# Attention items in tile order instead of block order, in a one-core diffusion backbone on Trainium2

## The chip, the cores and the metric

The program runs on one core of one Trainium2 chip. TensorE (PE) multiplies, VectorE (DVE) and ScalarE (ACT) work on the results, GpSimd (POOL) does a few small steps, and SyncE (SP) issues the DMAs. Each engine has a queue of its own that it works through in order; they wait for each other at semaphores. The metric is the time of one execution on the device in microseconds, as the median of the runs.

## The reference, cut to what matters

The reference runs two token streams, 512 latent tokens and 128 context tokens, through four layers. Layers 0 and 3 mix tokens by attention, layer 1 by pooling, layer 2 by a Fourier transform, and each layer ends with a gated ConvFFN. Here only the attention core matters:

```python
def attend_block(qb, keys, values, masks, sink):        # qb: 128 queries
    for kp, mk in zip(keys, masks):
        s = jnp.einsum('bqkgd,bskd->bkgqs', qb, kp) * scale
        if mk is not None: s = jnp.where(mk, s, NEG_INF)
        scores.append(s)
    m = max(sink, max of all scores); denom = exp(sink - m)
    for s, vp in zip(scores, values):
        p = jnp.exp(s - m[..., None])
        denom = denom + jnp.sum(p, axis=-1)
        out = out + jnp.einsum('bkgqs,bskd->bqkgd', p, vp)
    return out / denom
```

There are 16 query heads and 4 key heads of 64 channels. A block of 128 latent queries sees its own block of keys, its neighbours (with a band mask of width 128) and 128 cached context keys. The block of context queries sees only the 128 context keys. The output of the attention goes through a 1024 x 1024 matrix (`attn_w_o`) into the residual stream.

## The kernel before

All activations lie transposed: 1024 channels in 8 tiles of 128 partitions, 642 columns (512 latent, 128 context tokens, and two extra columns). A weight matrix is taken in units of one output tile. Each unit is a sum over 8 (or 11) input tiles, and each input tile is five matmuls on split values (L607 to L611), so that the products are as exact as in fp32.

The attention core of a layer is 40 items: 8 query tiles of two heads each, times 5 blocks of queries (`nb` 0 to 3 latent, `nb` 4 context). `WORK` (L382) lists them, and item `w` of the layer (counted from 0 in this text) is looked up in it by every engine. Before the change the list runs over the tiles within a block: items 0 to 7 are block 0, and so on, and items 32 to 39 are the context block. The size of an item is set by its block alone. `BLOCKS` (L381) holds the key blocks: three for `nb` 0 and 3, four for `nb` 1 and 2, one for `nb` 4. This text calls them 3-block, 4-block and 1-block items. A tile thus has two 3-block, two 4-block items and one 1-block item.

An item goes through a pipeline that is written out by hand, one step of the loop per item and engine, in these orders:

- PE, step w (L876 to L898): `scores(w+1)` (L830, L833), `values(w-3)` (L861), `turn(w-1)`, which transposes the probabilities (L846). In layer 0, for even w from 4 to 30, it multiplies one chunk of the modulation weights as well (`ada_multiply`, L747), and at w = 34 it turns the collected rows (`ada_turn`, L757).
- DVE, step w (L1765 to L1776): `masked(w)` adds the mask and takes the maximum (L1737, twice, then L1744 and L1745), `normed(w-1)` divides by the sum (L1753, then L1755 for two heads), `out_lo(w-4)` makes the low part of the output (L1762). In layer 0 it also copies and adds the modulation rows at w = 33 and 35 (L1408, L1415).
- ACT, step w (L1227 to L1233): `exps(w)` (L1207), `out_hi(w-3)` (L1224), `turned(w-1)` copies the transposed probabilities out of PSUM (L1218).
- POOL puts the sink into a spare column of each probability tile (L589).

The waits that matter: `scores(w+1)` wants `masked(w-1)` finished (L820), since the scores have two pairs of PSUM banks. `masked(w)` wants its scores (L1735). `turn(w-1)` wants `normed(w-1)` (L840). `values(w-3)` wants the output bank free (L853, L854): layer 3 has two output banks (`out_bank`, L413), so the low part of item w-5 must be done; layer 0 has one, since the other holds the modulation sums, so the low part of item w-4 must be done, and DVE does that at the end of its own step w.

The first unit of the output matrix is begun inside the loop. `first_output(kk)` (L866) multiplies input tile kk, and `FIRST_OUTPUT` (L65) says after which step: tiles 0 to 2 at step 39, 3 and 4 at 40, 5 at 41, 6 and 7 at 42. It waits for the low parts of the items that it reads (L871): in block order tile kk is complete with item 32 + kk. The DVE waits once per tile for the scales of the query heads (L1742), in the first eight items.

Of the kernel before, what the change touches and what calls it, by code (L numbers as in the profile page):

```python
# [29 lines left out]
KT = D // P  # L30
# [31 lines left out]
FIRST_PAIRS = FIRST_CHUNKS // 2  # L62
FIRST_BATCHES = FIRST_PAIRS + 1
X_PARTS = ((0, 2), (2, 4), (4, 8))
FIRST_OUTPUT = {39: (0, 1, 2), 40: (3, 4), 41: (5,), 42: (6, 7)}  # L65
IDLE_TILES = {"pool": 17, "fnet": 23}
UP_ROWS = 10
DOWN_PAIRS = (8, 6)
# [37 lines left out]
def build(nc, t):  # L106
    with ExitStack() as ctx:
# [3 lines left out]
        def sem(name):  # L111
            return ctx.enter_context(nc.semaphore(name))
# [181 lines left out]
        ol_made = sem("ol_made")  # L294
# [84 lines left out]
        CACHED = (384, 384, 384, 0)  # L379
        SPAN = ((128, 512), (0, 512), (0, 512), (0, 384), (128, 256))  # L380
        BLOCKS = ((1, 2, 3), (0, 1, 2, 3), (0, 1, 2, 3), (0, 1, 2), (1,))  # L381
        WORK = [(nb, tile) for nb in range(5) for tile in range(KT)]  # L382

        def turns_in(layer, half):

# [161 lines left out]
        def _(pool):  # L547
# [14 lines left out]
            for layer in range(DEPTH):  # L562
                for second in (False, True):
# [9 lines left out]
                    if KINDS[layer] == "attn" and not second:  # L573
# [6 lines left out]
                        for w in range(w0, w0 + 40):  # L580
                            nb, tile = WORK[w - w0]
                            end = SPAN[nb][1]
# [12 lines left out]
        def _(pe):  # L595
            def products(par, kk, b, first, last, plain=False):


                main, wide = ps[:, 2 * par, 0:MAIN], ps[:, 2 * par + 1, :]
                wh, wl = w_hi[par][:, kk, :], w_lo[par][:, kk, :]  # L600
                if plain:
                    for n, (w, part) in enumerate(((wh, 0), (wh, 1), (wl, 0))):
                        pe.matmul(main, w, b[:, part, 0:MAIN], start=(first and n == 0), stop=(last and n == 2))  # L603
                        mm = pe.matmul(wide[:, 0:TAIL], w, b[:, part, MAIN:NT], start=(first and n == 0),  # L604
                                       stop=(last and n == 2))
                    return mm
                pe.matmul(main, wh, b[:, 0, 0:MAIN], start=first, stop=False)  # L607
                pe.matmul(main, wh, b[:, 1, 0:MAIN], start=False, stop=False)  # L608
                pe.matmul(wide, wh, b[:, :, MAIN:NT], start=first, stop=last, skip_group_check=True)  # L609
                pe.matmul(main, wl, b[:, 0, 0:MAIN], start=False, stop=last)  # L610
                return pe.matmul(wide[:, 0:TAIL], wl, b[:, 0, MAIN:NT], start=False, stop=last,  # L611
                                 skip_group_check=True)
# [28 lines left out]
            def h_tiles(kk):  # L641
                return h[:, kk, :, :]
# [144 lines left out]
            for layer, kind in enumerate(KINDS):  # L787
# [5 lines left out]
                if kind == "attn":  # L793
# [20 lines left out]
                    w0 = 40 * a  # L814

                    def scores(w):
                        nb, tile = WORK[w - w0]
                        ga = tile // 4
                        if w - w0 >= 2:
                            pe.wait_ge(max_made, w - 1)  # L820
                        if w - w0 < 2:
                            wait_taken(pe, u0 + 10 + w - w0)
                        pe.wait_ge(qk_ready, 10 * a + tile + 3)
                        for hd in range(2):
                            rows = slice(HD * hd, HD * hd + HD)
                            q = qkv[rows, Q0 + tile, TOKEN_BLOCKS[nb]:TOKEN_BLOCKS[nb] + P]
                            out = ps[:, 2 * (w % 2) + hd, :]
                            lo, hi = KEYS[nb]
                            first = TOKEN_BLOCKS[FIRST_KEYS[nb]]
                            mm = pe.matmul(out[:, lo:hi], q, qkv[rows, K0 + ga, first:first + hi - lo],  # L830
                                           start=True, stop=True)
                            if nb < 4:
                                mm = pe.matmul(out[:, CACHED[nb]:CACHED[nb] + P], q, ck[rows, ga, :],  # L833
                                               start=True, stop=True)
                            mm.then_inc(s_done, 1)

                    def turn(w):
                        nb, _ = WORK[w - w0]
                        for hd in range(2):
                            pe.wait_ge(p_ready, 2 * w + hd + 1)  # L840
                            if w == w0:
                                pe.wait_ge(q_root, KT * (a + 1))
                            if w - w0 >= 1:
                                pe.wait_ge(pt_made, 2 * (w - 1) + hd + 1)
                            for b in BLOCKS[nb]:
                                mm = pe.transpose(ps[:, 4 + hd, b * P:(b + 1) * P],  # L846
                                                  prob[w % 3][:, hd, b * P:(b + 1) * P], ident[:])
                            mm.then_inc(t_done, 1)

                    def values(w):  # L850
                        nb, tile = WORK[w - w0]
                        ga = tile // 4
                        if w - w0 >= 2 or (w > w0 and layer == 0):  # L853
                            pe.wait_ge(ol_made, w - 1 if layer else w)  # L854
                        pe.wait_ge(pt_made, 2 * w + 2)
                        for b in BLOCKS[nb]:
                            for hd in range(2):
                                kv = slice(HD * (2 * ga + hd), HD * (2 * ga + hd + 1))
                                own = KEYS[nb][0] <= b * P < KEYS[nb][1]
                                v = v_tok[:, FIRST_KEYS[nb] + b - KEYS[nb][0] // P, kv] if own else cv[:, kv]  # L860
                                mm = pe.matmul(out_bank(layer, w)[HD * hd:HD * hd + HD, :], v,  # L861
                                               probT[w % 3][hd][:, b * P:(b + 1) * P],
                                               start=(b == BLOCKS[nb][0]), stop=(b == BLOCKS[nb][-1]))
                        mm.then_inc(o_done, 1)

                    def first_output(kk):  # L866

                        if kk == 0:
                            pe.wait_ge(lo_made, u0 + 13)
                            pe.wait_ge(max_made, w0 + 39)  # L870
                        pe.wait_ge(ol_made, w0 + 4 * KT + kk + 1)  # L871
                        mm = products(0, kk, h_tiles(kk), kk == 0, kk == KT - 1)
                        if kk == KT - 1:
                            mm.then_inc(unit_done, 1)

                    scores(w0)  # L876
                    for w in range(w0, w0 + 43):
# [17 lines left out]
                        if layer == 0 and w == 34:  # L895
                            ada_turn(FIRST_BATCHES, ADA_SHARED)
                        for kk in FIRST_OUTPUT.get(w - w0, ()):
                            first_output(kk)  # L898
# [126 lines left out]
        def _(act):  # L1025
# [140 lines left out]
            for layer, kind in enumerate(KINDS):  # L1166
                u0 = UNIT0[layer]
                norm(layer, False, KT if layer == 0 else 0 if explicit(layer, False) else KT - 1)
                if kind == "attn":
# [30 lines left out]
                    def exps(w):  # L1200
                        nb, tile = WORK[w - w0]
                        lo, hi = SPAN[nb]
# [8 lines left out]
                    def turned(w):  # L1211
                        nb, _ = WORK[w - w0]
                        b0, b1 = BLOCKS[nb][0] * P, (BLOCKS[nb][-1] + 1) * P
# [176 lines left out]
        def _(dve):  # L1390
# [254 lines left out]
            for layer, kind in enumerate(KINDS):  # L1645
# [9 lines left out]
                if kind == "attn":  # L1655
# [69 lines left out]
                    w0 = 40 * a  # L1725

                    def masked(w):

                        nb, tile = WORK[w - w0]
                        ga, r = tile // 4, tile % 4  # L1730
                        lo, hi = SPAN[nb]
                        if w - w0 >= 3:
                            dve.wait_ge(t_done, 2 * (w - 2))
                        for hd in range(2):
                            dve.wait_ge(s_done, 2 * w + hd + 1)  # L1735
                            st = stat[:, w % 2, hd, :]
                            own.link(dve.tensor_tensor_reduce(  # L1737
                                out=prob[w % 3][:, hd, lo:hi], in0=ps[:, 2 * (w % 2) + hd, lo:hi],
                                in1=band[:, (0 if nb == 3 else P) + lo:(0 if nb == 3 else P) + hi], scale=1.0, scalar=-3e38, op0=ALU.add, op1=ALU.max,
                                accum_out=st[:, 0:1]))  # L1740
                        st, head = stat[:, w % 2, :, :], 8 * ga + r
                        if w - w0 < KT:  # L1742
                            dve.wait_ge(q_scaled, KT * a + tile + 1)
                        own.link(dve.tensor_tensor(st[:, :, 1], st[:, :, 0], neg_scale[:, tile, nb, :], ALU.mult))  # L1744
                        dve.tensor_tensor(st[:, :, 1], st[:, :, 1], neg_sink[:, a, head:head + 5:4],  # L1745
                                          ALU.min).then_inc(max_made, 1)
# [314 lines left out]
```

## Time and profile before

| what | value |
|---|---|
| median of 3 runs | 2638.93 us (2638.85 to 2640.75) |
| the profiled execution, its own time | 2638.25 us |
| its span in the trace | 2636.6 us |
| PE busy | 2588.3 us, 98% of the span |
| DVE busy | 1977.9 us, 75% |
| ACT busy | 1297.0 us, 49% |
| POOL busy | 112.1 us, 4% |
| granted PE clock, mean | 0.994 |
| attention core of layer 0 | about 138 to 279 us of the span |
| attention core of layer 3 | about 1990 to 2112 us of the span |

Times are microseconds of the span. A row of the timeline gives the start, the duration, the engine, the line and the operation; "x8" means that eight such instructions in a row are shown as one. Where the engine had been idle, the row ends with the idle time and what ended it. PEld is the weight load of a matmul, which runs beside the matmul before it. An instruction of DVE in the timeline can start a little before the one before it has ended, so costs are best read from start to start.

### The profile page before, as it was taken

What the parts mean: (1) busy time and instruction counts of PE and PEld (TensorE: products, weight loads), DVE (VectorE), ACT (ScalarE), POOL (GpSimd) and SP (SyncE); (2) the same over time, 40 slices, a digit from 0 to 9 for tenths busy, and PEclk for the clock granted to TensorE, in tenths of its full rate; (3) what the DMA queues carried; (4) which work ended last, traced back from release to release, by engine and by line L of the source; (5) the groups of instructions that cost most, each with busy time, mean ns of one, the idle gap of its engine ahead of it and who ended that gap; (6) DMA issues with size and microseconds to landing.
All of it is one profiled execution on the core that took longest, in us unless ns stands there. A gap on an engine that the chain in (4) does not pass through costs nothing.

```text
span 2636.6 us, 43707 instructions
## 1 busy us (share of the span) xinstructions
PE 2588.3 (98%) x16114; PEld 2402.8 (91%) x16114; DVE 1977.9 (75%) x3735; ACT 1297.0 (49%) x2285; POOL 112.1 (4%) x145
## 2 busy tenths in 40 slices
PE   7999999999999999999999999999999999999999
PEld 6966899999999999999989999999997799999998
DVE  4687488888895888888856888888868857754772
ACT  4478365325525662455245661454347846633551
POOL 2000100000012000000101000000100010000000
PEclk9999999999999999999999999999999999999999
DMA  7233223443341335334302334334320022222222
GB/s 296 64 119 128 76 94 119 147 149 107 131 144 50 115 120 179 128 111 150 119 17 81 104 130 169 122 110 156 112 63 29 2 64 73 72 87 65 80 84 76
DMA packets 72565, 279.69 MB, mean 106 GB/s; under 512 B 7920, under 2 KB 11376, under 8 KB 68848
## 3 DMA queue, kind: packets, MB, share of 16 engines
q1 hardware_dynamic: 72432, 277.93, 31.2%
q8 instruction: 81, 1.33, 0.2%
q14 instruction: 52, 0.43, 0.1%
HBM read 274.75 MB, written 3.15 MB: 105 GB/s over the span
## 4 chain that ended last, share of the span: by engine, by line
PE 45%; DVE 3%; issue 1%; ACT 1%; POOL 0%; DVEq 0%; ACTq 0%
PE ps L609 11%; PE ps L607 8%; PE ps L608 8%; PE ps L610 8%; PE ps L611 6%; PE ps L846 1%; PE ps L861 1%; PE ps L830 1%; DVE h L1509 1%; PE ps L679 1%; DVE ada_w L1455 0%; PE ps L953 0%; PE ps L603 0%; DVE h L1506 0%; DVE prob L1737 0%
## 5 line engine op out<-in xcount | busy, mean ns | idle before, releaser
L609 PE MATMUL ps<-h,w_hi 128*128 128x512 f32 x1768 | 699.6, 396 | 0.0
L607 PE MATMUL ps<-h,w_hi 128*128 128x386 f32 x1768 | 605.4, 342 | 9.1 <-DVE h L1509 8.7
L608 PE MATMUL ps<-h,w_hi 128*128 128x386 f32 x1768 | 602.2, 341 | 0.0
L610 PE MATMUL ps<-h,w_lo 128*128 128x386 f32 x1768 | 598.0, 338 | 0.0
L1036 ACT ACTIVATE tail<-ps 128x256 f32<-128x256 f32 x281 | 108.4, 386 | 948.8 <-PE ps L611 948.2
L611 PE MATMUL ps<-h,w_lo 128*128 128x256 f32 x1768 | 502.9, 284 | 0.0
L611 PEld LDWEIGHTS ps<-h,w_lo 128*128 128x128 f32 x1768 | 333.1, 188 | 79.4
L1396 DVE TENSOR_TENSOR w_lo<-w_raw,w_hi 128x1024 fp32r<-128x1024 f32 (+1 forms) x288 | 377.6, 1311 | 7.8 <-DMA cv<-in_cache_v 3.4
L607 PEld LDWEIGHTS ps<-h,w_hi 128*128 128x128 f32 x1768 | 338.9, 192 | 14.5 <-DVE h L1509 12.7
L608 PEld LDWEIGHTS ps<-h,w_hi 128*128 128x128 f32 x1768 | 335.3, 190 | 0.0
L1031 ACT ACTIVATE w_hi<-w_raw 128x1024 fp32r<-128x1024 f32 (+1 forms) x288 | 323.8, 1124 | 22.0 <-PE ps L604 15.3
L609 PEld LDWEIGHTS ps<-h,w_hi 128*128 128x128 f32 x1768 | 333.5, 189 | 0.0
L610 PEld LDWEIGHTS ps<-h,w_lo 128*128 128x128 f32 x1768 | 333.3, 189 | 0.0
L1587 DVE TENSOR_TENSOR scaled<-ps,rstd 128x386 f32<-128x386 f32 x200 | 112.0, 560 | 213.8 <-PE ps L611 213.6
L609 PE MATMUL ps<-f,w_hi 128*128 128x512 f32 x660 | 260.7, 395 | 0.0
L1617 DVE SCALAR_TENSOR_TENSOR x<-ps,mods,x 128x385 f32<-128x385 f32 (+2 forms) x102 | 58.0, 580 | 230.0 <-PE ps L611 206.7
L607 PE MATMUL ps<-f,w_hi 128*128 128x386 f32 x660 | 224.5, 340 | 2.6 <-DVE w_lo L1396 2.6
L608 PE MATMUL ps<-f,w_hi 128*128 128x386 f32 x660 | 223.7, 339 | 0.0
L610 PE MATMUL ps<-f,w_lo 128*128 128x386 f32 x660 | 223.2, 338 | 0.0
L1322 ACT ACTIVATE u_pad<-scaled 128x512 f32<-128x512 f32 x352 | 178.8, 556 | 37.1 <-DVE scaled L1589 32.5
L611 PE MATMUL ps<-f,w_lo 128*128 128x256 f32 x660 | 187.0, 283 | 0.0
L1327 ACT ACTIVATE conv_out<-u_pad,conv 128x642 f32<-128x642 f32 x176 | 163.1, 927 | 32.9 <-ACT u_pad L1322 31.3
(183 smaller groups left out, 3915.5 us busy)
## 6 DMA issues: line engine op xcount, KB each, us to landing
w_raw<-in_w_in SPq DMA_DIRECT2D x176, 512.0 KB, 3.6
w_raw<-in_w_out SPq DMA_DIRECT2D x64, 704.0 KB, 4.1
ada_w<-in_ada_t SPq DMA_DIRECT2D x42, 1024.0 KB, 6.3
row_w<-in_ada_t SPq DMA_DIRECT2D x60, 512.0 KB, 3.6
ada_w<-in_ada_w SPq DMA_DIRECT2D x18, 1024.0 KB, 5.1
w_raw<-in_w_qkv SPq DMA_DIRECT2D x24, 512.0 KB, 3.6
w_raw<-in_w_o SPq DMA_DIRECT2D x16, 512.0 KB, 3.5
first_w<-in_ada_w SPq DMA_DIRECT2D x6, 1024.0 KB, 15.0
```

Of the source, the lines that this page charges most:

```text
L607: pe.matmul(main, wh, b[:, 0, 0:MAIN], start=first, stop=False)
L608: pe.matmul(main, wh, b[:, 1, 0:MAIN], start=False, stop=False)
L609: pe.matmul(wide, wh, b[:, :, MAIN:NT], start=first, stop=last, skip_group_check=True)
L610: pe.matmul(main, wl, b[:, 0, 0:MAIN], start=False, stop=last)
L611: return pe.matmul(wide[:, 0:TAIL], wl, b[:, 0, MAIN:NT], start=False, stop=last, skip_group_check=True)
L1031: act.activation(w_hi[par][:, 0:k, :], w_raw[par][:, 0:k, :], ACT.Copy).then_inc(hi_made, 1)
L1036: act.activation(tail[par][:], ps[:, 2 * par + 1, TAIL:2 * TAIL], ACT.Copy).then_inc(tail_copied, 1)
L1322: op = act.activation(u_pad[par][:, at + 1:at + 1 + n], scaled[par][:, at:at + n], ACT.Identity, bias=scaled[par][:, SHIFT_AT[cnd]:SHIFT_A ...
L1327: act.activation(conv_out[par][:], u_pad[par][:, 1:NT + 1], ACT.Identity, bias=conv[:, v, 3:4] if isint else conv[:, bass.ds(v, 1), 3], sc ...
L1396: dve.tensor_tensor(w_lo[par][:, 0:k, :], w_raw[par][:, 0:k, :], w_hi[par][:, 0:k, :].bitcast(F32), ALU.subtract).then_inc(lo_made, 1)
L1587: dve.tensor_tensor(scaled[par][:, 0:MAIN], ps[:, 2 * par, 0:MAIN], rstd[:, 0:MAIN], ALU.mult)
L1617: op = dve.scalar_tensor_tensor(xt, src, gt, xt, ALU.mult, ALU.add)
```

## The change

The list of items runs over the blocks within a tile, so every fifth item is a context item, and tile kk of the output is complete with item 5 kk + 4. Two waits are rewritten for the new order, without changing what they guard. The product of input tile 6 is made one step earlier, at step 41.

```diff
-FIRST_OUTPUT = {39: (0, 1, 2), 40: (3, 4), 41: (5,), 42: (6, 7)}
+FIRST_OUTPUT = {39: (0, 1, 2), 40: (3, 4), 41: (5, 6), 42: (7,)}
@@ the list of items
-        WORK = [(nb, tile) for nb in range(5) for tile in range(KT)]
+        WORK = [(nb, tile) for tile in range(KT) for nb in range(5)]
@@ first_output, on PE
-                        pe.wait_ge(ol_made, w0 + 4 * KT + kk + 1)
+                        pe.wait_ge(ol_made, w0 + 5 * (kk + 1))
@@ masked, on DVE
-                        if w - w0 < KT:
+                        if nb == 0:
                             dve.wait_ge(q_scaled, KT * a + tile + 1)
```

## Rows read from the trace of the kernel before

**Rows 1.** Windows: stretch, length, busy PE, PEld, DVE, ACT, POOL, granted clock, DMA.
```profile
2092.00:2101.00 9.00, 7.82 (x59) 4.51 (x59) 8.30 (x52) 8.22 (x38) 0.77 (x4) 0.83 0.01 2
2101.00:2104.00 3.00, 3.00 (x10) 2.89 (x11) 1.16 (x6) 1.17 (x7) 0.00 (x0) 0.50 0.03 5
269.00:272.00 3.00, 3.00 (x11) 2.86 (x11) 0.66 (x3) 0.65 (x3) 0.00 (x0) 0.55 0.00 0
```

**Rows 2.** Timeline of layer 0, 4-block items: start, duration, engine, line, operation.
```profile
191.39 0.16 DVE L1745 TENSOR_TENSOR stat<-stat,neg_sink 128x2 f32<-128x2 f32 x1
...
191.57 0.92 PE L830 MATMUL ps<-qkv 64*128 64x384 f32 x4
191.66 0.88 DVE L1755 TENSOR_SCALAR prob<-prob,stat 128x512 f32<-128x512 f32 x2
...
192.46 0.28 DVE L1762 TENSOR_TENSOR h<-ps,h 128x128 fp32r<-128x128 f32 x1
192.80 0.64 PEld L861 LDWEIGHTS ps<-probT,v_tok 128*64 128x64 f32 x12 [0.28 <-DVE h L1762]
...
192.85 0.69 DVE L1737 CUSTOM_DVE_ANT_0 prob<-ps,band 128x512 f32<-128x512 f32 x1
...
193.82 1.09 PE L846 MATMUL ps<-ident,prob 128*128 128x128 f32 x8
...
194.51 0.16 DVE L1745 TENSOR_TENSOR stat<-stat,neg_sink 128x2 f32<-128x2 f32 x1
...
194.85 1.07 PE L747 MATMUL ps<-ada_w,cond_act 128*32 128x256 f32 x16
...
195.84 0.31 PEld L830 LDWEIGHTS ps<-qkv 64*128 64x128 f32 x4 [0.41 <-issue]
...
196.92 0.64 PEld L861 LDWEIGHTS ps<-probT,v_tok 128*64 128x64 f32 x12
```

**Rows 3.** Timeline of layer 3, PE, 1-block items.
```profile
2091.14 0.44 PE L846 MATMUL ps<-ident,prob 128*128 128x128 f32 x2
...
2091.51 0.49 PE L830 MATMUL ps<-qkv 64*128 64x128 f32 x4
...
2091.93 0.44 PE L861 MATMUL ps<-probT,cv 128*64 128x128 f32 x4
```

**Rows 4.** Timeline of layer 3, DVE, 1-block items.
```profile
2097.18 0.48 DVE L1755 TENSOR_SCALAR prob<-prob,stat 128x128 f32<-128x128 f32 x2
...
2097.57 0.28 DVE L1762 TENSOR_TENSOR h<-ps,h 128x128 fp32r<-128x128 f32 x1
...
2097.77 0.28 DVE L1737 CUSTOM_DVE_ANT_0 prob<-ps,band 128x128 f32<-128x128 f32 x1
...
2098.63 0.16 DVE L1745 TENSOR_TENSOR stat<-stat,neg_sink 128x2 f32<-128x2 f32 x1
```

**Rows 5.** Timeline, L1745 of items 1 and 39: layer 0, then layer 3.
```profile
149.79 0.17 DVE L1745 TENSOR_TENSOR stat<-stat,neg_sink 128x2 f32<-128x2 f32 x1
...
267.18 0.16 DVE L1745 TENSOR_TENSOR stat<-stat,neg_sink 128x2 f32<-128x2 f32 x1
...
2002.36 0.17 DVE L1745 TENSOR_TENSOR stat<-stat,neg_sink 128x2 f32<-128x2 f32 x1
...
2100.35 0.17 DVE L1745 TENSOR_TENSOR stat<-stat,neg_sink 128x2 f32<-128x2 f32 x1
```

**Rows 6.** Timeline of layer 0: the turn of the modulation rows on PE.
```profile
259.62 0.53 PEld L757 LDWEIGHTS ps<-pick,ada_rows 128*128 128x128 f32 x4
```

**Rows 7.** Timeline of layer 3: values of item 39 and what follows them.
```profile
2109.59 0.44 PE L861 MATMUL ps<-probT,v_tok 128*64 128x128 f32 x4
2109.96 0.19 PEld L607 LDWEIGHTS ps<-h,w_hi 128*128 128x128 f32 x1 [0.17 <-issue]
...
2110.39 0.29 DVE L1762 TENSOR_TENSOR h<-ps,h 128x128 fp32r<-128x128 f32 x1 [1.16 <-ACT h L1224]
```

**Rows 8.** Timeline of layer 0: first product of the output matrix.
```profile
269.08 0.34 PEld L607 LDWEIGHTS ps<-h,w_hi 128*128 128x128 f32 x1
```

## Prediction

> **What bounds the kernel now.** PE is busy for 98% of the span in the table above, so PE sets the time of every unit of weights, and the change doesn't touch those. It touches two stretches of about 140 and 120 us, the attention cores of layers 0 and 3. I read these in the timeline, start to start, and found two regimes. Among the 4-block items PE has no gap but issue gaps. Among the 1-block items at the end of the core, DVE sets the pace and PE waits: in 9 us it is busy for 7.82 us, and half of that already runs on a falling clock; the granted clock over the stretch is 0.83 [rows 1]. Right behind it the output products start at a clock of 0.50 in layer 3 and 0.55 in layer 0 [rows 1], the lower of the two levels (1.2 of 2.4 GHz). So PE waits in the short items, and pays again behind them.
>
> **The cost of one item.** From the 4-block and 1-block rows, in us:
> - PE scores: 195.84 to 196.92, 1.08 [rows 2]; 1-block 0.42 [rows 3].
> - PE turn: 193.82 to 194.85, 1.02 [rows 2]; 0.37 [rows 3]. PE values: 192.80 to 193.82, 1.02 [rows 2]; 0.37 [rows 7].
> - DVE, from the start of the two L1755 to L1762 ("normed"): 0.80 [rows 2]; 0.39 [rows 4].
> - DVE, mask and maximum up to L1745 ("masked"): 192.85 to 194.51, 1.66 [rows 2]; 2097.77 to 2098.63, 0.86 [rows 4].
> - DVE, from L1762 to the next mask: 0.20 [rows 4].
> - DVE, from L1745 to L1755: 0.27 [rows 2], taken as 0.28.
> - Start of scores to start of their mask: 191.57 to 192.85, 1.28 [rows 2], that is scores plus 0.20.
>
> For 3-block items, which have no rows here, I interpolate by the number of blocks: scores 0.86, turn 0.80, values 0.80, normed 0.66, masked 1.39. One tile has one 1-block, two 3-block, two 4-block items. DVE then works 2 x (1.39 + 0.66) + 2 x (1.66 + 0.80) + 0.86 + 0.39 + 5 x 0.48 = 12.67 us per tile, PE 2 x 2.46 + 2 x 3.12 + 1.16 = 12.32, in either order. ACT has the same instructions in either order as well; in the 1-block stretch it is busy for 8.22 us where DVE is for 8.30 [rows 1], so it is close behind, and I leave it out of the walk. The change removes and adds no instruction. All it can do is change who waits.
>
> **Walking the waits.** Let m(w) be the start of L1745 of item w. I carried three rules forward from item to item:
> - DVE: L1762 of item w-4 starts at m(w) + 0.28 + normed(w-1). The next mask starts 0.20 later, or at the scores' start plus 1.28, 1.06 or 0.62, whichever is later. m(w+1) follows by masked(w+1).
> - PE in step w: scores(w+1), values(w-3), turn(w-1), plus 1.00 for a modulation chunk (194.85 to 195.84 [rows 2]) where layer 0 has one. turn(w-1) not before m(w) + 0.28 plus the first head's readiness, 0.56, 0.48 or 0.34.
> - Layer 0 only: values(w-3) not before L1762 of item w-4 plus 0.34 (192.46 to 192.80, the 0.28 wait in the row [rows 2]).
>
> The readiness is an estimate: half of normed plus a handover. It is bounded by 0.34 and 0.84 (the whole of normed).
>
> On the old order the walk starts at item 1. Layer 3: 2002.36 leads to item 39 at 2100.43, and the row says 2100.35. Layer 0: 149.79 leads to 266.33, and the row says 267.18 [rows 5]; the walk leaves out the copy of the modulation rows, their turn, and the falling clock there. So the rules describe the order before to within 0.1 us where nothing else acts.
>
> On the new order item 1 has four blocks, 0.27 more, so the start is later by that.
>
> | core, order | item 1 | item 31 | item 39 | PE done with turn(38) |
> |---|---|---|---|---|
> | layer 3 before | 2002.36 | 2086.00 | 2100.43 | 2101.42 |
> | layer 3 after | 2002.63 | 2079.99 | 2100.56 | 2102.13 |
> | layer 0 before | 149.79 | 250.21 | 266.33 | 268.08 |
> | layer 0 after | 150.06 | 245.05 | 267.67 | 270.83 |
>
> The new order is 5 to 6 us ahead at item 31, since its cheap items have come earlier, and loses all of it in the last eight, which are now of all sizes. The reason that it doesn't win is a ring of waits that goes once through each tile. **Layer 3:** from m of the second 3-block item, 0.28 + 0.56, turn of the 4-block item before it 1.02, scores 0.86, values 1.02, turn 0.80, to the 4-block scores' start; then 1.28, masked 1.66, and on DVE to the next two items, 2.80 + 2.67. That is 12.95 against 12.67 of DVE alone: 0.28 per tile. **Layer 0:** the ring waits for the one output bank instead: 0.28 + 0.80 + 0.34, values 0.80, turn 1.02, then the same: 14.3 us per tile where no chunk is due. The old order in its like-sized items has nothing of the kind: two 1-block items need 3.4 us on DVE, and the bank wait is shorter than that.
>
> PE pays for it in layer 0: two tiles with five chunks come to 32.4 us in the walk against 24.6 + 5 = 29.6 of work.
>
> **The end of the core.** PE's tail behind turn(38) has eight products of the output tile, turn(39) and values(37) to values(39). The new order has a 4-block item at 37 (1.02 - 0.37 = 0.65 more) and a 3-block item at 38 (0.43 more). Tile 7's product now stands directly behind values(39). Its operand is done by L1762 at 2110.39, which is 0.80 after the values' start at 2109.59; plus 0.34 makes 1.14, while PE is free after 0.37 [rows 7]. So PE waits 0.77. Before, tile 6's product covered this. That product has moved to step 41, where PE had no wait either, so the move gains nothing. Sum 1.85 us per core. In layer 0 the turn of the modulation rows, 0.53 [rows 6], was beside a DVE-bound stretch and now lies in the ring: 0.53 more than the walk.
>
> **The clock.** In the walk PE is busy for 12.3 of 12.95 us (layer 3) and 12.3 of 14.3 (layer 0) to the end, where before the last eight items had it at 1.16 us of work in about 1.73. I take it that the clock holds. Then the products get back 3 us x (1 - 0.50) = 1.5 us in layer 3, and 3 x (1 - 0.55) = 1.35 in layer 0 [rows 1].
>
> **The sum.** Layer 3: turn(38) 0.71 later, + 1.85 - 1.5 = +1.1. Layer 0: before, the first product stands at 269.08 [rows 8]; after, 270.83 + 0.53 = 271.36, 2.3 later, + 1.85 - 1.35 = +2.8. Together +3.9. The reordered waits on DVE cost nothing: the scales of a tile are made before its first item in both orders, and the wait for item 5 (kk + 1) is met by 5 items or more except for tile 7. The profiled execution took 2638.25 us, so after would be 2642.2 on its scale; the median of the runs is 0.7 higher, which gives 2642.8. An error of 0.1 in the ring counts some fifteen times, and readiness by its bounds -0.2 to +0.3 in layer 3 alone, up to 2 us; so 2640.3 to 2645.3 for this case.
>
> **Rivals.**
> 1. **The clock falls all the same** (slower). PE in layer 0 has gaps of up to a microsecond in each ring, and full-sized items now stand where short ones stood. At the lower level PE's 12.3 us per tile become up to 24.6, and it would set the pace outright: a spell of 6 us, twice the stretches that the windows show [rows 1], would lose 6 x (1 - 14.3 / 24.6) = 2.5 us. One in each layer: 2642.8 + 5.0 = 2647.8. It decides if PE's waits in the last tiles are enough to lower the grant. Against it: the mean grant of 0.994 over the span, in the table above, leaves room for few falls. The Trainium skill, "TensorE: Matmul & The Clock Gate", section "A second HAM failure mode: psum-queue depth-cycling", tells of a kernel whose frequent short PE idles between groups made the clock swing between its levels; by it this rival would be the forecast. That page and the trace don't agree so far: the windows show the low level behind the sparsest stretch [rows 1]. Chance 0.15.
> 2. **The rings don't bind** (faster). If the engines can run further apart than the rules allow, PE fills its waits: 7 x 0.28 = 2.0 in layer 3, and in layer 0 3 x 2.6 for thirty items with chunks and 1.6 x 1.4 for the rest, 10.0. 2642.8 - 12 = 2631. Against it is the wait in the row of layer 0 [rows 2], and that the walk meets item 39. Chance 0.07.
> 3. **The order doesn't matter**: the waits lost and won cancel, or the ring is softer than I count because two-head instructions hand over halfway. 2638.9 within 1.4. Chance 0.18.
> 4. The forecast: 0.60, with a quarter of it above 2644.2.
>
> **How the numbers follow.** A measurement of this kernel tells apart about 0.2%, 5.3 us, so "same" is 2633.7 to 2644.2. Slower: 0.15 + 0.15 = 0.30. Faster: 0.07. Same: 0.63. The range leaves out rival 2 and part of rival 1: 2637.5 to 2648.
>
> **What would show it.** L1745 of item 31 near 2080 and 245, and of item 39 near 2100.6 and 268. Every fifth step of PE in layer 0 waits at L861 for L1762, and tile periods are near 12.95 (layer 3) and 14.3 (layer 0, last items). The first output products run at a grant of 1.00. A wait of about 0.8 us stands before the last of them. The forecast is wrong if the grant is below 1.00 in a core, if ACT turns up as the releaser of L1753 or L1762, or if the tile period of layer 3 is DVE's 12.67.

## The result, and the profile after

The changed kernel took 2644.64 us in the median of 12 runs (2640.01 to 2648.69), the kernel before 2638.99 us (2634.99 to 2640.75, also 12). The ratio is 1.0019, with an interval of 1.0011 to 1.0028: 5.65 us between the medians, or about 5.0 by the ratio, so right at the 5.3 up to which the prediction says "same". The forecast of 2642.8 is 1.8 us too low. A second measurement of the same pair gave 2643.64 against 2640.15 us, ratio 1.0015 (1.0005 to 1.0025). So the change costs 0.15 to 0.2%: both intervals lie above 1, so it doesn't gain.

The profiled execution of after took 2644.01 us with a span of 2642.4 us, 5.8 more than before. Its page has as many instructions on each engine as before. PE is busy for 3.4 us less, PEld for 3.3 and DVE for 3.0 less, ACT for 1.3 more:

```profile
PE 2584.9 (98%) x16114; PEld 2399.5 (91%) x16114; DVE 1974.9 (75%) x3735; ACT 1298.3 (49%) x2285; POOL 112.0 (4%) x145
```

The windows at the ends of the two cores show why (stretch, length, busy PE, PEld, DVE, ACT, POOL, granted clock, DMA), first layer 0, then layer 3:

```profile
265.00:271.00 6.00, 4.84 (x51) 3.57 (x48) 5.58 (x26) 5.52 (x16) 0.65 (x2) 1.00 0.00 0
271.00:274.00 3.00, 2.74 (x31) 2.33 (x32) 1.38 (x6) 2.58 (x10) 0.00 (x0) 1.00 0.03 5
274.00:277.00 3.00, 3.00 (x22) 2.66 (x22) 0.59 (x3) 0.78 (x2) 0.00 (x0) 1.00 0.00 0
...
2102.00:2108.00 6.00, 5.57 (x63) 4.28 (x60) 5.65 (x26) 5.88 (x17) 0.19 (x1) 1.00 0.02 5
2108.00:2111.00 3.00, 3.00 (x20) 2.77 (x18) 0.97 (x5) 1.59 (x7) 0.00 (x0) 1.00 0.00 0
```

Where the old order had a grant of 0.83, then 0.50 and 0.55 [rows 1], the new one has 1.00 throughout, and twice the matmuls in the 3 us behind the items (x20 and x22 against x10 and x11). Nevertheless the cores are longer. I measure a core from its first scores to the start of the second output unit (the first L607 of it), in us of each profile:

| | layer 0: item 1, item 39, first product, end | length | layer 3: item 1, item 39, first product, end | length |
|---|---|---|---|---|
| before | 149.79, 267.18, 269.15, 279.35 | 141.37 | 2002.36, 2100.35, 2101.31, 2111.84 | 121.32 |
| after | 152.80, 270.80, 273.90, 284.80 | 144.08 | 2009.28, 2106.90, 2108.28, 2119.14 | 121.96 |

That is +2.71 and +0.64 us. The other 2.4 of the 5.8 us lie outside: the core of layer 0 starts 2.74 later, the stretch between the cores is 1.21 longer, and what follows layer 3 is 1.5 shorter. No instruction differs there. The table gives the starts of the matmuls; a weight load starts up to 0.1 earlier.

### The profile page after: what moved, and what is told of

The parts are those of the page before. It is cut to its first block, busy times and chain, and to the rows that moved or that the text cites. A ratio compares the mean times of both kernels' runs of the same rounds, so it can differ in the third digit from the quotient of the medians.

```text
span 2642.4 us, 43707 instructions
## 1 busy us (share of the span) xinstructions
PE 2584.9 (98%) x16114; PEld 2399.5 (91%) x16114; DVE 1974.9 (75%) x3735; ACT 1298.3 (49%) x2285; POOL 112.0 (4%) x145
## 4 chain that ended last, share of the span: by engine, by line
PE 43%; DVE 5%; issue 1%; ACT 1%; DVEq 0%; POOL 0%; ACTq 0%
PE ps L609 11%; PE ps L607 8%; PE ps L608 8%; PE ps L610 8%; PE ps L611 6%; DVE prob L1737 1%; PE ps L846 1%; DVE h L1509 1%; PE ps L679 1%; DVE prob L1755 0%; PE ps L830 0%; PE ps L861 0%; DVE ada_w L1455 0%; PE ps L953 0%; PE ps L603 0%
## 5 line engine op out<-in xcount | busy, mean ns | idle before, releaser
L607 PE MATMUL ps<-h,w_hi 128*128 128x386 f32 x1768 | 604.6, 342 | 10.7 <-DVE h L1509 8.9
L607 PEld LDWEIGHTS ps<-h,w_hi 128*128 128x128 f32 x1768 | 338.2, 191 | 16.5 <-DVE h L1509 11.5
L607 PE MATMUL ps<-f,w_hi 128*128 128x386 f32 x660 | 224.5, 340 | 2.6 <-DVE w_lo L1396 2.5
```

## The experiments

**1. The changed kernel once more (tile_order_again).** No edit; it asks whether the lengths of the cores repeat.

> The changed kernel once more, for a second profile and a closer interval. Theory: the two attention cores, from the first scores to the end of the first output unit, cost 2.7 us more in layer 0 and 0.6 us more in layer 3 than in the kernel before (141.4 to 144.1 us and 121.3 to 122.0 us in the first profiles), and this doesn't vary; the rest of the measured 5.6 us comes from stretches whose instructions are the same in both kernels, above all the start of the program, where the granted clock varies from run to run. Expected: cores at 144.1 and 122.0 us within 0.2, time within 3 us of 2643. Rival: the granted clock falls inside a core of the new order in some runs; then a core is over 1 us longer and has a window below 1.00.

The cores took 144.13 and 121.99 us, within 0.05 of the first profile, and the granted clock is 1.00 over both. What doesn't repeat is the rest: span less both cores is 2376.4 us in the first profile and 2372.4 in this one. Three windows of each, after first, show where it differs:

```profile
45.00:60.00 15.00, 13.37 (x83) 12.08 (x76) 7.12 (x18) 4.40 (x8) 0.00 (x0) 0.66 0.67 250
...
330.00:350.00 20.00, 18.63 (x105) 17.44 (x104) 13.98 (x31) 15.61 (x31) 3.60 (x2) 0.91 0.23 79
800.00:820.00 20.00, 19.91 (x145) 19.56 (x144) 8.88 (x21) 7.23 (x12) 1.53 (x1) 0.91 0.36 139
```

```profile
45.00:60.00 15.00, 12.31 (x88) 10.82 (x82) 7.17 (x18) 4.40 (x8) 0.00 (x0) 0.77 0.70 252
...
330.00:350.00 20.00, 18.63 (x113) 17.43 (x112) 15.46 (x33) 15.54 (x32) 3.60 (x2) 1.00 0.24 79
800.00:820.00 20.00, 19.68 (x161) 19.28 (x160) 9.75 (x22) 9.37 (x16) 0.00 (x0) 1.00 0.24 89
```

The same stretches run at 0.91 in one profile and at 1.00 in the next. From here on I judge by the lengths of the cores.

**2. One output bank in layer 3, in either order (tile_one_bank, block_one_bank).** The forecast says that in layer 0 the single output bank makes a ring of 14.3 us per tile in the new order, and that the old order has nothing of the kind. Layer 3 has two banks. If the reason is right, giving it one must lengthen the new order's core by far more than the old one's.

```diff
-            return ps[:, 6 + (w % 2 if layer else 0), 0:P]
+            return ps[:, 6, 0:P]
...
-                        if w - w0 >= 2 or (w > w0 and layer == 0):
-                            pe.wait_ge(ol_made, w - 1 if layer else w)
+                        if w > w0:
+                            pe.wait_ge(ol_made, w)
```

> The new order, with one output bank in layer 3 as layer 0 has it (values wait for the low part of the item just before). Theory: the ring of waits through each tile grows from 12.9 to 14.3 us, so layer 3's core is 10.4 us longer (122.0 to 132.4 us), and PE waits at the values for L1762. Rival: the rings don't bind, the two queues drift apart as they like; then the core is longer by less than 3 us.

> The old order, with one output bank in layer 3. Theory: in the old order the wait for the bank costs less, 6.0 us for the core (121.3 to 127.3 us), as like-sized items follow each other. With tile_one_bank this tells how much dearer the bank wait is in the new order: 4.4 us. Rival: the bank wait costs the same in both orders (the order is then not what makes layer 0 slower).

Layer 3 took 132.64 us in the new order (+10.7; ratio of the whole to the kernel before 1.0058, 1.0040 to 1.0077) and 128.29 in the old one (+7.0; 1.0023, 1.0009 to 1.0038). The maxima (L1745) of one item and of the same item one tile later, in the new order:

```profile
2062.92 0.16 DVE L1745 TENSOR_TENSOR stat<-stat,neg_sink 128x2 f32<-128x2 f32 x1
...
2077.25 0.16 DVE L1745 TENSOR_TENSOR stat<-stat,neg_sink 128x2 f32<-128x2 f32 x1
```

14.33 us per tile, as the ring has it. The waits of layer 3 (who waited for whom, us in total, times, longest), new order first, then old:

```profile
PEld ps L861 <- DVE h L1762: 17.5, 23, 1.0
PE ps L861 <- DVE h L1762: 13.1, 23, 0.8
```

```profile
PEld ps L861 <- DVE h L1762: 12.0, 25, 1.2
PE ps L861 <- DVE h L1762: 6.3, 15, 1.0
```

The bank costs the new order 3.7 us more than the old. But it costs the old one 7.0 as well, so two thirds of its price are paid in either order. The old order's result is 1.0 above what was expected. From item 1 to item 39 it takes 103.57 us, 5.6 more than in the kernel before; the excess lies behind the items, where the clock is at the lower level:

```profile
2110.00:2116.00 6.00, 5.55 (x23) 4.30 (x22) 2.22 (x12) 2.57 (x12) 0.00 (x0) 0.50 0.02 4
```

The kernel before has such a spell too, and it is as long (0.50 from 2098 to 2104). But there item 39 stands at 2100.35, and here at 2110.52, so that here the spell lies about 1.8 us later against the items, and more of it falls on the products, where PE sets the pace. At half the clock that is an estimated 0.9 us. That it is the 1.0 is likely and was not tested by itself. A second point goes against the first rival: with one bank the new order's PE waits for L1762 alone 13.1 us in 23 places of layer 3, and its clock stayed at 1.00 in both cores.

**3. The same extra work on the ring and off it (ring_on, ring_off).** In one item of each tile the last transpose of each head is done twice, to the same place. The work was put at 0.27 us per tile; in the traces it is less, for such a turn takes 1.02 us start to start where it took 0.81, so 0.21. Put into the 3-block item of nb 3, it lies on the ring as the forecast walks it; put into that of nb 0, it lies off the ring in layer 3. Were PE's own sum the limit, or were the order without effect, the two kernels would be alike.

```diff
-                            for b in BLOCKS[nb]:
+                            for b in BLOCKS[nb] + (BLOCKS[nb][-1:] if nb == 3 else ()):
```

> The new order, with the last transpose of each head done twice for the items of block 3 (a 3-block item, whose turn lies on the ring of waits): 0.27 us more PE work per tile. Theory: the ring gets longer by that, eight times, in both layers: cores 2.2 us longer than the new order's (146.3 and 124.2 us). Rival: DVE or the sum of PE's work bounds a tile; then the same addition costs the same wherever it stands, in block 3 or in block 0.

> The same addition, 0.27 us of PE work per tile, for the items of block 0 (also 3-block, whose turn has slack). Theory: nothing in layer 3 (122.0 us); in layer 0 with its chunks and single bank 0.9 us (145.0 us). Rival: as much as in block 3.

On the ring the cores became 1.79 and 1.84 us longer than after's (layer 0, layer 3), off it 0.75 and 0.1. Each kernel was run once, with the grant at 1.00 over both cores. The period of a tile in layer 3, first with the work on the ring, then off it:

```profile
2076.20 0.16 DVE L1745 TENSOR_TENSOR stat<-stat,neg_sink 128x2 f32<-128x2 f32 x1
...
2089.35 0.17 DVE L1745 TENSOR_TENSOR stat<-stat,neg_sink 128x2 f32<-128x2 f32 x1
```

```profile
2074.30 0.17 DVE L1745 TENSOR_TENSOR stat<-stat,neg_sink 128x2 f32<-128x2 f32 x1
...
2087.24 0.16 DVE L1745 TENSOR_TENSOR stat<-stat,neg_sink 128x2 f32<-128x2 f32 x1
```

13.15 against 12.94 us. Off the ring the added work disappears in layer 3: the period is that of after, 12.92. So there is a ring in layer 3, it passes through the turn of nb 3 and not through that of nb 0, and what is added on it comes through whole: 0.23 us per tile for about 0.21 of work. That the cores grew by 1.8 and not by the expected 2.2 is the work put too high, and not slack in the ring.

**4. Tile 6's product back behind the loop's last step (tile_six_late).** The change moved it one step forward. The forecast said that this gains nothing and counted the uncovered wait of tile 7 at 0.77 us.

```diff
-FIRST_OUTPUT = {39: (0, 1, 2), 40: (3, 4), 41: (5, 6), 42: (7,)}
+FIRST_OUTPUT = {39: (0, 1, 2), 40: (3, 4), 41: (5,), 42: (6, 7)}
```

> The new order with the product of input tile 6 back at step 42, as before. Theory: the product then covers the wait of tile 7's product for item 39, so the wait of 0.8 us at the end of each core goes and each core is 0.8 us shorter (143.3 and 121.2 us). Rival: the move is free, cores unchanged.

The cores took 143.33 and 121.24 us, 0.75 and 0.72 less than after's. The end of layer 3 in the timeline (start, duration, engine, line, operation, in brackets idle before it and releaser), first of after:

```profile
2117.01 0.20 PEld L861 LDWEIGHTS ps<-probT,v_tok 128*64 128x64 f32 x4 [0.20 <-issue]
...
2117.81 0.29 DVE L1762 TENSOR_TENSOR h<-ps,h 128x128 fp32r<-128x128 f32 x1 [2.03 <-ACT h L1224]
2118.15 0.19 PEld L607 LDWEIGHTS ps<-h,w_hi 128*128 128x128 f32 x1 [0.94 <-DVE h L1762]
```

and with tile 6 late:

```profile
2113.21 0.20 PEld L861 LDWEIGHTS ps<-probT,v_tok 128*64 128x64 f32 x4 [0.20 <-issue]
2113.58 0.19 PEld L607 LDWEIGHTS ps<-h,w_hi 128*128 128x128 f32 x1 [0.17 <-issue]
...
2114.01 0.29 DVE L1762 TENSOR_TENSOR h<-ps,h 128x128 fp32r<-128x128 f32 x1 [1.15 <-ACT h L1224]
...
2114.45 0.19 PEld L607 LDWEIGHTS ps<-h,w_hi 128*128 128x128 f32 x1
```

In after it is 1.14 us from the load of the last values to tile 7's product, of which the values' matmuls fill 0.44. With tile 6 between them, the low part is ready at 2114.30 and tile 7 starts at 2114.45 with no wait. The whole took 2641.09 us, ratio to the kernel before 1.0003 (0.9994 to 1.0012). So this one entry, 1.5 us in two cores, is a good part of what the change costs. Without it the order can't be told from the old one by the whole time; by its cores it is still 1.9 us longer, all of it in layer 0.

**5. The old order with PE kept busy in the context items (block_busy, block_busy_again).** The 1-block items' transposes are written twice to the same place, which gives PE more to do in items that DVE paces (the turn of such an item takes 0.58 us start to start, before 0.37). If the low grant at the ends of the old cores comes from PE's waits, it should vanish, and its cost with it.

```diff
-                            for b in BLOCKS[nb]:
+                            for b in BLOCKS[nb] * (2 if nb == 4 else 1):
```

> The old order, with the transposes of the context items done twice, so that PE waits less at the end of a core (1.53 us of work in 1.73 instead of 1.16). Theory: the low granted clock behind the context items comes from PE's waits in them; it stays at 1.00 now, which gives back 1.4 to 1.5 us, less 0.5 to 0.9 for the added work at the end: cores 140.9 and 120.3 us against 141.4 and 121.3. Rival: the grant falls there for another reason or at random; then windows below 1.00 remain and the cores are longer than before.

> The old order with the context items' transposes done twice, a second time on the same chip as mix_two. Theory: the low grant behind the context items is gone in every run, cores 140.2 and 120.1 us, and the time is below the kernel before by about 2.4 us, the sum of the two cores' differences. Rival: its gain in the first look came from the start of the program and not from the cores; then a second profile shows a grant below 1.00 at the end of a core.

The cores took 140.18 and 120.09 us, and 140.13 and 120.10 the second time; before has 141.37 and 121.32. The windows of the first:

```profile
264.00:270.00 6.00, 4.73 (x39) 3.26 (x40) 4.93 (x32) 5.42 (x24) 0.39 (x2) 1.00 0.00 0
270.00:276.00 6.00, 6.00 (x39) 5.04 (x38) 0.64 (x4) 1.07 (x5) 0.00 (x0) 1.00 0.00 0
2092.00:2098.00 6.00, 5.39 (x46) 3.37 (x44) 5.51 (x36) 5.58 (x28) 0.58 (x3) 1.00 0.00 1
2098.00:2104.00 6.00, 5.33 (x35) 4.79 (x36) 2.08 (x11) 2.41 (x11) 0.00 (x0) 1.00 0.02 4
```

The grant stays at 1.00, and each core gains 1.2 us by more work. That is net of the added transposes, of which those behind the last items stand in PE's own path. The whole took 2635.76 us against 2639.34, ratio 0.9983 (0.9974 to 0.9993), and 0.9986 (0.9978 to 0.9995) when repeated.

**6. The kernel before once more (block_order_again).** This asks whether the low grant in the old order is there each time.

> The kernel before once more, for a second profile. Theory: cores 141.4 and 121.3 us, each with the low grant at its end. Rival: the fall at the end of a core was a chance of the first profile; then a core without it is 1.4 us or more shorter.

The cores took 141.30 and 121.31 us, and the grant is low at both ends again:

```profile
264.00:270.00 6.00, 4.65 (x32) 2.58 (x30) 5.27 (x33) 5.33 (x23) 0.58 (x3) 0.80 0.02 3
270.00:276.00 6.00, 5.23 (x25) 4.27 (x25) 1.76 (x9) 2.11 (x9) 0.00 (x0) 0.63 0.00 0
2098.00:2104.00 6.00, 4.88 (x30) 2.75 (x29) 5.55 (x35) 5.34 (x24) 0.39 (x2) 0.72 0.01 3
2104.00:2110.00 6.00, 6.00 (x29) 5.36 (x29) 1.15 (x6) 1.59 (x8) 0.00 (x0) 0.72 0.01 3
```

Three profiles of the old order (with block_one_bank) have it at both ends of their cores; six of the new order have it at neither.

**7. What the walk proposes (mix, mix_two).** By the walk, layer 0 should keep the old order with experiment 5's transposes. For layer 3 I walked other orders inside a tile; 1, 2, 4, 0, 3 leaves DVE no ring to wait for. Tile 6's product is back at step 42 in both layers, and the waits for the low parts and for the scales follow the new lists.

```diff
-        WORK = [(nb, tile) for nb in range(5) for tile in range(KT)]
+        WORK = {0: [(nb, tile) for nb in (0, 1, 2, 3, 4) for tile in range(KT)],
+                3: [(nb, tile) for tile in range(KT) for nb in (1, 2, 4, 0, 3)]}
...
-                            for b in BLOCKS[nb]:
+                            for b in BLOCKS[nb] * (2 if nb == 4 else 1):
```

> Layer 0 in the old order, with the transposes of the context items done twice; layer 3 in tile order, but with the blocks of a tile in the order 1, 2, 4, 0, 3, and the product of input tile 6 at step 42. Theory: with this order within a tile no ring is longer than DVE's 12.67 us by more than a little; the rules of the walk give a core 3.75 us shorter than the changed kernel's in layer 3, 118.2 us, and 140.9 in layer 0. Together 3.6 us less than the kernel before. Rival: the new order is slow by itself, not by a ring through blocks 2 and 3; then layer 3 stays at 121.2 or more.

Layer 0 took 140.20 us, as before in experiment 5. Layer 3 took 120.54, 2.3 more than expected, with a tile period of 12.85 where 12.67 was expected. The edit had left the doubled transposes in layer 3 too, where they are on PE's path; walked with them, the core comes to 120.8. mix_two has them in layer 0 alone (`nb == 4 and layer == 0`).

> As the run before (layer 0 in the old order with the transposes of the context items doubled, layer 3 in tile order with blocks 1, 2, 4, 0, 3), but with nothing doubled in layer 3. In the run before the doubling had been left in layer 3, where the context item's turn lies on a ring of this order; with 0.37 us more there the walk gives 120.8 us (120.5 measured). Theory: without it the tile period is DVE's own, 12.67 us, and the core of layer 3 is 118.2 us; layer 0 stays at 140.2. Rival: another bound holds the tile period at 12.85; then the core is 119.5 us or more.

Layer 3 took 118.99 us, and its period is DVE's own (this kernel's L1748 is L1745):

```profile
2060.24 0.16 DVE L1748 TENSOR_TENSOR stat<-stat,neg_sink 128x2 f32<-128x2 f32 x1
...
2072.88 0.16 DVE L1748 TENSOR_TENSOR stat<-stat,neg_sink 128x2 f32<-128x2 f32 x1
```

12.64 us. The core is 0.8 longer than the walk has it, though its tiles keep the walk's pace (12.64 against 12.67), so the 0.8 lies mostly at its two ends. The whole took 2633.24 us against 2639.32, ratio 0.9983 (0.9974 to 0.9993); mix had 2636.19 and 0.9992 (0.9983 to 1.0001). This is the fastest kernel of the study by its cores (259.1 us in two, before 262.7, after 266.0). By the ratio it can't be told from block_busy.

## Why the prediction was right, and where it was not

**The walk.** Item 31 of layer 3 and items 37 to 39, L1745 in the timeline of after:

```profile
2086.40 0.16 DVE L1745 TENSOR_TENSOR stat<-stat,neg_sink 128x2 f32<-128x2 f32 x1
...
2102.11 0.16 DVE L1745 TENSOR_TENSOR stat<-stat,neg_sink 128x2 f32<-128x2 f32 x1
2104.77 0.16 DVE L1745 TENSOR_TENSOR stat<-stat,neg_sink 128x2 f32<-128x2 f32 x1
2106.90 0.17 DVE L1745 TENSOR_TENSOR stat<-stat,neg_sink 128x2 f32<-128x2 f32 x1
```

From item 1 (2009.28) it is 77.12 us to item 31 and 97.62 to item 39; the walk had 77.36 and 97.93. In layer 0 item 31 stands at 247.85, 95.05 behind item 1, where the walk had 94.99. The rest of the way to item 39 took 22.95; the walk had 22.62, plus 0.53 for the turn of the modulation rows, so that term came to about 0.3. The new order is ahead at item 31 (77.12 us from item 1 against 83.64 before, in layer 3) and loses it again in the last eight, as forecast.

**The rings.** Layer 3's period is 12.92 us per tile (12.95 forecast, DVE's own work 12.67), and experiment 3 shows the ring's path. In layer 0 two tiles with their chunks take 32.43 us (item 6 to item 16, 166.83 to 199.26), where the walk had 32.4. The bare 14.3 can't be read there: the last tile, from item 31 to 36, takes 15.36 (247.85 to 263.21), with the last chunk and the turn of the modulation rows in it. In layer 0 the turned wait is in the timeline of after, at the end of a tile:

```profile
252.39 0.28 DVE L1762 TENSOR_TENSOR h<-ps,h 128x128 fp32r<-128x128 f32 x1
252.73 0.20 PEld L861 LDWEIGHTS ps<-probT,v_tok 128*64 128x64 f32 x4 [0.93 <-DVE h L1762]
```

The handover is the 0.34 of [rows 2], and PE has waited 0.93 us in a place where the 4-block row waited 0.28. Summed over layer 0 the waits are, before first and then after:

```profile
DVE prob L1737 <- PE ps L833: 16.2, 14, 1.4
PEld ps L861 <- DVE h L1762: 10.3, 20, 1.2
PE ps L861 <- DVE h L1762: 5.6, 11, 1.0
```

```profile
DVE prob L1737 <- PE ps L833: 19.3, 19, 2.3
PEld ps L861 <- DVE h L1762: 13.7, 16, 1.3
PE ps L861 <- DVE h L1762: 10.6, 15, 1.1
```

Loads wait at L861 16 times instead of 20, and 3.4 us longer in sum. The forecast named every fifth step as the place; there are 16 such waits for eight tiles, two in a tile. DVE then waits longer for its scores, up to 2.3 us at once, and that is how PE's wait reaches the bound engine. Experiment 2 moves this ring to layer 3 and gets its 14.33 us. It also shows one sentence of the forecast to be wrong: that the old order has nothing of the kind. There too the loads wait for L1762 in layer 0 (20 times, 10.3 us), and the one bank costs it 7.0 us in layer 3. The sum was not harmed, since it takes layer 0's old order as measured.

**The end of the core.** The wait before tile 7's product was forecast as 1.14 us from the values, and is 1.14. Its cost was in the sum. But the sentence that the move gains nothing stops short: the move is what uncovers the wait, it loses 0.75 us per core, and it should have been priced as a loss of its own, apart from the order. One of the signs named for an error was badly chosen: ACT (L1224) does release L1762, but only for items 37 to 39, where it also does in the order before [rows 7], and ACT (L1207) releases L1753 once in each core, at the last item, in both orders. So it tells nothing.

**The clock.** It holds in the new order, as forecast. What that gives back is best read from the first two products of the output matrix, start to start of their first loads. In layer 3 they take 3.22 us before (2101.24 to 2104.46) and 1.75 after (2108.25 to 2110.00), so 1.47; in layer 0 2.97 before (269.08 to 272.05) and 1.76 after (273.87 to 275.63), so 1.21. The forecast took 1.5 and 1.35. Experiment 5's 1.2 us per core agrees, as it is what is left when the added transposes are paid. One reading was off: of the 9 us in the first row of [rows 1] not half, but the last 3.1 run at the lower level (from 2097.9 on), and they cost nothing there: items 36 to 39 follow each other at 1.73 us, before the fall and behind it.

**The sum.** Layer 0: +2.71 measured, +2.8 forecast. Layer 3: +0.64 against +1.1. The start is as forecast (item 1 later by 0.26, forecast 0.27). From item 1 to 39 it is 0.37 shorter than before (forecast 0.14), and behind item 39 it is 0.76 longer (forecast 0.93). Together +3.35 in both profiles (within 0.1) against +3.9. The term that was not foreseen is the rest of the program. The forecast carried it over unchanged, and it was 2.4 us longer in the first profile of after and 1.5 us shorter in the second. So what the medians show beyond the cores' 3.4 us (2.2 in the first measurement, 0.1 in the second) is within the spread of that part. That none of it is systematic isn't shown, and without its 2.2 us the first median would lie well inside "same".

**The rivals.** (1) The clock falls all the same: refuted. In layer 0 PE is busy for 4.84 of 6 us ahead of the products and the grant is 1.00, and so in all six profiles of that order, with one bank in layer 3 too. The Trainium skill, "TensorE: Matmul & The Clock Gate", section "A second HAM failure mode: psum-queue depth-cycling", tells of a kernel in which frequent short idles of PE between groups of matmuls make the clock swing, and taken as a rule it would have made this the forecast. For the new order the trace disagrees (1.00); for the short items of the old one it agrees (0.50 behind them, and 1.00 once they hold more work). (2) The rings don't bind: refuted by experiments 2 and 3, and by the cores, which would then be shorter than before's. (Its 2.6 us for two tiles in layer 0 is 2.8 by the prediction's own 32.4 and 29.6, which makes it 10.6 and not 10.0.) (3) The order doesn't matter: refuted by the same, though with tile 6 left in its place it comes to that in the whole time (1.0003): the ring of layer 3 and the clock cancel, and only layer 0 stays longer.

## What to carry to other kernels

When in-order queues that wait for each other are given the same work in another order, the sums of the engines don't move; find the ring of waits that the new order closes, add up what lies on it, and compare that with the busiest engine's sum. That sizes are mixed doesn't decide it: the same items in the order 0, 1, 2, 3, 4 of a tile closed a ring of 12.92 us, and in the order 1, 2, 4, 0, 3 they ran at DVE's own 12.64. Price each entry of a hand-written schedule by itself as well: here one product moved by one step made 1.5 of about 3.4 us.

## What the runs showed of the hardware

Work that computes nothing new made the kernel faster: doubled transposes in the last eight items kept the grant at 1.00 behind them and gave 1.2 us per core, twice. PE busy for 4.84 of 6 us in the new order and for 4.73 in experiment 5 kept it. In the kernel before it was busy for 5.49 of the 6 us from 2091 to 2097, at a grant of 1.00, and within the next microsecond the grant fell. (Windows that hold part of the low spell can't be compared with these, since the same matmuls are busy for longer in them.) So the busy share of such a stretch doesn't tell whether the grant will hold.

The grant also falls elsewhere, now here and now there, in both orders (0.91 from 800 to 820 in before, and the windows of experiment 1 for the new order), and the whole time follows it. Of the 12 runs of after, the two with a mean grant of 0.999 took 2640.0 and 2640.3 us, the four with 0.996 or 0.997 took 2640.8 to 2644.0, and the six with 0.995 took 2645.3 to 2648.7. This spread of 8.7 us is larger than the change's whole effect. With it in the way, an edit of 1 us can be read in the length of its stretch, and not in the time.
